# Token mixing of a two-block float32 layer stack: bonus products, off-block mask and output norm placed on GpSimd

## The reference, cut to what matters

```python
S = S * w_t + sa[..., None] * (kk_t * a_t) + v_t[..., None] * k_t      # the recurrence, token by token
y = ((y - mean) * rsqrt(var + 64e-5)).reshape(B, T, RW_WIDTH)          # norm of each head's 64 outputs
y = y * ln_x_w + ln_x_b
bonus = jnp.sum(r4 * k4 * r_k, axis=-1, keepdims=True) * v4            # one number per head and token, times v
y = (y + bonus) * g                                                    # g: the gate
```

## Time and profile before

| | |
|---|---|
| median of 3 runs | 3659.44 us (3657.07 to 3661.78) |
| the profiled execution | 3660.92 us, its span 3658.8 us |
| TensorE busy | 3543.9 us, 97% of the span |
| VectorE busy | 2155.3 us, 59% |
| ScalarE busy | 1755.6 us, 48% |
| GpSimd busy | 346.0 us, 9% |
| mean granted clock of TensorE over the span | 0.984 |
| token mixing's rounds | about 280 to 800 us of the span |

### The profile page before, as it was taken

How to read it: one execution, slowest core, us unless ns; L and a number is a source line. 1 busy time by engine, 2 the same in 40 slices (tenths; PEclk the granted TensorE clock), 3 DMA queues, 4 the chain that set the end, 5 groups by cost and what they waited for, 6 DMA issues and landing times. The chain is left out here.

```text
span 3658.8 us, 50852 instructions
## 1 busy us (share of the span) xinstructions
PE 3543.9 (97%) x20474; PEld 3010.5 (82%) x20474; DVE 2155.3 (59%) x2871; ACT 1755.6 (48%) x2613; POOL 346.0 (9%) x217
## 2 busy tenths in 40 slices
PE   8899999989999999999999999999999999999999
PEld 6777677678799999888899998887788887788777
DVE  4676556645566488555544465555687885555454
ACT  5454333324444478444444444444655554444753
POOL 0001000000059700000000000000022210000000
PEclk9999999999999999999999999999999999999999
DMA  6454234445545455555555565554533335455334
GB/s 224 157 183 153 97 137 141 146 169 199 199 168 179 178 171 180 186 211 188 190 207 184 207 254 193 219 191 176 182 141 138 133 132 186 176 195 185 127 138 161
DMA packets 112140, 638.57 MB, mean 175 GB/s; under 512 B 18698, under 2 KB 24618, under 8 KB 40152
## 3 DMA queue, kind: packets, MB, share of 16 engines
q1 hardware_dynamic: 106664, 622.98, 47.8%
q0 software_dynamic: 5296, 13.15, 1.1%
HBM read 611.10 MB, written 21.54 MB: 173 GB/s over the span
## 5 line engine op out<-in xcount | busy, mean ns | idle before, releaser
L222 DVE TENSOR_TENSOR lo_w<-ring,hi_w 128x1024 fp32r<-128x1024 f32 x500 | 612.6, 1225 | 987.4 <-ACT hi_w L216 979.2
L216 ACT CAST hi_w<-ring 128x1024 fp32r<-128x1024 f32 x540 | 569.8, 1055 | 954.2 <-DMA ring<-in_wstream 929.8
L224 DVE TENSOR_TENSOR lo_w<-ring,hi_w 128x1024 fp32r<-128x1024 f32 x500 | 612.3, 1225 | 0.0
L1997 PE MATMUL PS<-hi_x,lo_w 128*128 128x256 f32 x2048 | 580.1, 283 | 0.0
L1997 PE MATMUL PS<-hi_x,hi_w 128*128 128x256 f32 x2048 | 576.3, 281 | 3.0 <-POOL lo_w L224 3.0
L1997 PE MATMUL PS<-lo_x,hi_w 128*128 128x256 f32 x2048 | 571.4, 279 | 0.0
L217 ACT CAST hi_w<-ring 128x1024 fp32r<-128x1024 f32 x540 | 565.5, 1047 | 0.0
L2023 PE MATMUL PS<-hi_w,hi_g 128*128 128x512 f32 x1024 | 404.0, 395 | 1.3 <-issue 1.3
L2023 PE MATMUL PS<-lo_w,hi_g 128*128 128x512 f32 x1024 | 403.5, 394 | 0.0
L2023 PE MATMUL PS<-hi_w,lo_g 128*128 128x512 f32 x1024 | 403.2, 394 | 0.0
L1997 PEld LDWEIGHTS PS<-hi_x,hi_w 128*128 128x128 f32 x2048 | 389.2, 190 | 3.5 <-ACT GG L2237 3.4
(11 more groups left out here) (581 smaller groups left out, 5777.0 us busy)
## 6 DMA issues: line engine op xcount, KB each, us to landing
ring<-in_wstream SPq DMA_DIRECT2D x540, 1024.0 KB, 4.8
other_G<-staged SPq DMA_DIRECT2D x32, 256.0 KB, 6.1
hot<-other_G SPq DMA_DIRECT2D x8, 1024.0 KB, 6.9
gates_dram<-gst POOLq DMA_DIRECT2D x8, 512.0 KB, 4.8
x_dram<-x SPq DMA_DIRECT2D x2, 2048.0 KB, 12.0
x<-x_dram SPq DMA_DIRECT2D x2, 2048.0 KB, 9.4
prev<-RKV POOLq DMA_DIRECT2D x6, 508.0 KB, 5.2
x<-in_x SPq DMA_DIRECT2D x4, 512.0 KB, 6.6
```

The lines of the kernel that those rows point to most:

```text
L216: a.copy(hi_w[s][:, 0:HALF], ring[s][:, 0:HALF]).then_inc(S(f"hi{s}"), 1)
L222: v.tensor_tensor(lo_w[s][:, 0:HALF], ring[s][:, 0:HALF], hi_w[s][:, 0:HALF].bitcast(F32), ALU.subtract)
L224: v.tensor_tensor(lo_w[s][:, HALF:UNIT], ring[s][:, HALF:UNIT], hi_w[s][:, HALF:UNIT].bitcast(F32), ALU.subtract)\
L1997: m = nc.tensor.matmul(PS[:, s, 0:T], wa[s][:, k * P:(k + 1) * P], xa[:, k, :], start=(k == 0 and p == 0), stop=(k == KC - 1 and p == 2))
```

## The change

GpSimd computes the two bonus products of every round (`bonus_terms`, at the whole unit from offset 2.5), applies the mask (`off_block`, now in GpSimd's queue right behind `clear`, ahead of the gate copy or shift of the same unit), and, for rounds 0 to 2, computes the norm's five products and sums (`norm_lines`, at the whole unit from offset 16.25). On VectorE, `bonus` keeps the sum per head and moves from offset 4 to 7.25, behind the solve; the second half of the norm becomes `deviation` (a reciprocal, at the old place) and `gate_y` (the product with the gate, at offset 19.75, which is 7.75 of the next round). Round 3 keeps `finish`. The transpose of round 2's output moves from unit 77 to unit 80 on TensorE, ScalarE and VectorE, and the load of the second half of the norm's lines on SyncE from unit 66 to 68.

```diff
@@ SyncE
                 if u == 66:
                     gups(1)
+                if u == 68:
                     lines(1)
@@ TensorE
-                    if u == WIN + 1 and g < 3:
+                    if u == WIN + 1 and g < 2:
                         turn_y(g)
+                    if (u, g) == (WIN + 4, 2):
+                        turn_y(2)
@@ ScalarE
                     for n in late_due(U, g, 16, 13):
-                        a.wait_ge(S("gn_var"), n + 1)
+                        a.wait_ge(S("gn_var"), 2 * n + 1)
@@ GpSimd
+            def bonus_terms(n):
+                g.wait_ge(S("ends"), n + 1)
+                g.tensor_tensor(k4[:], k4[:], rkv_of(n)[0], ALU.mult)
+                g.drain()
+                g.tensor_tensor(k4[:], k4[:], par[:, 2, :], ALU.mult)
+                g.drain().then_inc(S("pool_terms"), 1)
+
+            def off_block(n):
+                g.wait_ge(S("rw_in"), 48)
+                g.tensor_tensor(LM[:, :, 0, :], LM[:, :, 0, :], offm[:].unsqueeze(1).broadcast_to((P, NH, P)), ALU.mult)
+                g.drain().then_inc(S("L_off"), 1)
+
+            def norm_lines(n):
+                r_, y_, v_ = rkv_of(n)
+                g.wait_ge(S("gn_var"), 2 * n + 2)
+                g.tensor_tensor(h3(r_), h3(v_), per_head(3 + n % 2), ALU.mult)
+                g.tensor_tensor(h3(y_), h3(y_), per_head(5), ALU.mult)
+                g.wait_ge(S("ln_in"), 32 * (n // 2) + 32)
+                g.drain()
+                g.tensor_tensor(y_, y_, lwlb[:, 0, :], ALU.mult)
+                g.drain()
+                g.tensor_tensor(y_, y_, lwlb[:, 1, :], ALU.add)
+                g.drain()
+                g.tensor_tensor(y_, y_, r_, ALU.add)
+                g.drain().then_inc(S("pool_terms"), 1)
...
                     if u == math.ceil(RB + RSTEP * n + 3.6):
                         steps_in(n)
                         clear(state_of(n, 1), "K_zero")
+                        off_block(n)
+                    if n < 3 and u == math.ceil(RB + RSTEP * n + 16.25):
+                        norm_lines(n)
+                    if u == math.ceil(RB + RSTEP * n + 2.5):
+                        bonus_terms(n)
                     if u == math.ceil(RB + RSTEP * n + 6.5):
                         steps_back(n)
@@ VectorE
             def bonus(n):
-                tt_(k4[:], k4[:], rkv_of(n)[0], ALU.mult)
-                v.drain()
-                tt_(k4[:], k4[:], par[:, 2, :], ALU.mult)
-                v.drain()
+                v.wait_ge(S("pool_terms"), (1, 2, 4, 6)[n])
                 v.tensor_reduce(s8[:, 3 + n % 2, :], h3(k4[:]), X, ALU.add)
                 v.drain().then_inc(S("bonus"), 1)
-            def off_block(n):
...
+            def deviation(n):
+                v.wait_ge(S("gn_std"), n + 1)
+                v.reciprocal(s8[:, 5, :], s8[:, 6, :])
+                v.drain().then_inc(S("gn_var"), 1)
+
+            def gate_y(n):
+                r_, y_, v_ = rkv_of(n)
+                v.wait_ge(S("pool_terms"), 2 * n + 3)
+                v.wait_ge(S("gt_ps"), n + 1)
+                tt_(r_, y_, PS[:, 3, :], ALU.mult)
+                v.drain().then_inc(S("y_done"), 1)
...
-                    for n in due(U, g, 4):
-                        bonus(n)
                     for n in late_due(U, g, 15.75, 12.75):
                         center(n)
                     for n in late_due(U, g, 16.25, 13.25):
-                        finish(n)
-                    for n in due(U, g, 5.25):
-                        off_block(n)
+                        if n < 3:
+                            deviation(n)
+                        else:
+                            finish(n)
                     for k in range(3):
                         for n in due(U, g, 6 + k / 4):
                             solve(n, k)
+                    for n in due(U, g, 7.25):
+                        bonus(n)
+                    for n in due(U, g, 19.75):
+                        if n < 3:
+                            gate_y(n)
...
-                    if U == WIN + 1 and g:
+                    if U == WIN + 1 and g in (1, 2):
                         turned_y(g - 1)
+                    if (U, g) == (WIN + 4, 3):
+                        turned_y(2)
```

More of the change, by code:

```diff
@@ L1606, in finish @@
                 v.wait_ge(S("gt_ps"), n + 1)
-                tt_(r_, y_, PS[:, 3 if n < 3 else 6, :], ALU.mult)
+                tt_(r_, y_, PS[:, 6, :], ALU.mult)
+                v.drain().then_inc(S("y_done"), 1)
[8 more added lines that the diff above has]
+                tt_(r_, y_, PS[:, 3, :], ALU.mult)
                 v.drain().then_inc(S("y_done"), 1)
```

## The result

The changed kernel takes 3682.65 us (median of 4, 3679.61 to 3685.88), the kernel before in the same comparison 3659.94 (median of 4). The ratio is 1.0061, with a 95% interval of 1.0048 to 1.0074: slower by 22.7 us. The profiled execution took 3683.94 us, with a span of 3682.1 and a granted clock of 0.981.

The account below looks back on a forecast made before the run. TensorE, busy 97%, was taken as the bound, waiting only where VectorE's bursts outlast the units split ahead. Rounds 0 to 3 summed as 3.9 + 4.3 + 7.3 + 1.0 = 16.5 us slower, 3676 on the median, range 3656 to 3689.

Parts of the forecast that it names:

- (c): Splits and solves: a 128x512 GpSimd product costs a two-input VectorE operation about 1.0 us, a 128x1024 one about 2.1.
- Whole-instruction exclusion: Skill's rule for GpSimd reads against two-input VectorE operations: each norm product would cost 1.3, the sum near 21 us.
- (c), last sentences: Later copy-in of norm lines on SyncE and copies back on GpSimd: microseconds to spare, closest in round 2.
- (a): Bonus reduction and previous round's gate moved behind the solve: 0.8 us each; costs 0.8, 0.5, 1.1 in rounds 0 to 2.
- The bonus products: On GpSimd they push one split by up to 1.0 us, ahead of a 1.2 TensorE wait: nothing.
- lost cover: If the 1.2 us TensorE wait covering the split delayed by bonus products were gone: 1.0 us a round.
- (b): Round 0's mask ahead of the shift's copy in GpSimd's queue: 3.1 us, bounds 2.4 and 4.2.
- Round 3: Freed time pays for mask and two products; three more cost 2.85, the missing turned block gives 0.85: 1.0 us later.
- No contention: Rival: GpSimd's turns fall into VectorE's idle time; +1.5 us, 3661, no change; chance 0.19.
- Faster: Rival: VectorE's own queue sets the solve's start, so freed time removes waits; 15 us less, 3644; chance 0.13.
- Worse: Rival: GpSimd runs at blocked length, norm outlasts the solve, and TensorE's clock falls after long waits; 3689; chance 0.08.
- likeliest case: Contention as summed over the four rounds: 16.5 us slower, own range 3667 to 3684; chance 0.60.

Follow-up runs that it names:

- pars_early: The changed kernel with SyncE's load of the second half's parameters waiting for GpSimd's bonus products instead of VectorE's sum; 3674.11 us, ratio 1.0037.
- round3_vector: The kernel before, nothing on GpSimd, with round 3's bonus and mask behind its solve and the third turned block moved as in the change; 3658.28 us, ratio 0.9990.
- norm_back: The changed kernel with the norm's second half back on VectorE for all rounds, GpSimd keeping bonus products and mask; 3665.09 us, ratio 1.0014.
- norm_writes: The changed kernel with GpSimd's five norm products and sums of rounds 0 to 2 replaced by memsets of the same tiles; 3662.52 us, ratio 1.0005.
- keys_late: The kernel before with round 3's bonus and mask behind its solve, and in rounds 1 to 3 keys_norm moved behind the spread; 3651.07 us, ratio 0.9974.

## Why the prediction was right, and where it was not

The direction and the mechanism held: slower, by contention in splits and solve. The sum was 16.5 us, measured was 22.7, of which 20.2 lie in the four rounds.

- *Contention, (c).* The forecast had 3, 4 and 3 held products in the solves of rounds 1, 2 and 3, at 0.95 each; there were 3, 3 and 1. The solves of rounds 1 and 2 took 12.8 us against 10.0 and 10.4, so about 0.9 and 0.8 each (a held product took 1.07 to 1.15, where the same one alone takes 0.18 to 0.22). Whole-instruction exclusion, the rule that was weighed there, describes what happens: a held product ends when GpSimd's operation ends. The price was nevertheless below the 1.29 of the operation: in the rows above VectorE spends the first part of each GpSimd operation in a reduction that is not held. The sum of near 21 us that this rule gave is closer than mine to the 20.2 of the rounds, but by chance: up to 4.8 us of the 20.2 come from the wait on SyncE, which is no contention. Round 2's stretch was forecast to lose 7.3 in all and lost 6.8; round 1, without the SyncE wait, 3.7 against 4.3. I named the solve at 13 to 14 us; it was a little less.
- *The missed wait, (c), last sentences.* The prediction looked at the norm lines on SyncE and not at `pars(1)`, which stands in the same queue and waits for `bonus`, the very signal that (a) moves from ahead of the solve to behind it. Everything behind `pars(1)` in that queue waited too, two ring loads among it. pars_early puts it at 3.1 us, and up to 1.7 more by the clock. This is the step of the prediction that failed.
- *The bonus products, put at nothing.* They cost 1.1 us in round 0: a split of 2.29 pushed `masked`, and TensorE waited. The price for a lost cover, 1.0 a round, was right; the cover was missing in round 0.
- *(b), 3.1 us for the mask in round 0.* The copy was issued some 2.8 us later against the start of the values, as forecast, but landed sooner: 4.2 us after its issue at 342.43, against 6.2 after 337.85 before. In the six kernels with the mask ahead of the shift the solve starts 22.4 to 24.3 us after the values (mean 23.4), in the seven others 21.8 to 22.8 (mean 22.3). So its place costs about 1.1 us, an estimate from two groups that overlap. The rest is made up by the copy: from its issue to VectorE's going on there were 4.2 to 5.7 us in the first group and 5.9 to 7.1 in the second; why is open. In the changed kernel itself the solve starts 0.8 later than before; with the sum's 0.8 and the late second shift's 1.0 this gives 2.6 of the 2.9 us that round 0's stretch lost. The 0.65 for a drain was also too much (0.17 here).
- *Round 3.* 1.0 forecast, 0.8 measured, and the bank wait of 10.8 lies in the 8 to 11 named. The two sides of the balance are real: the freed time is worth 2.9 in round3_vector, and the norm on GpSimd costs 2.2 by norm_back. How they were put together was not right, and that the sum fits is in part luck. The solve was to start 0.9 us earlier than before and to hold three products; measured from the values it starts 1.2 later, since the four split halves ahead of it lose some 5 us, and it holds one product, 0.9 us.
- *Rivals.* No contention is refuted by norm_writes against the changed kernel. Faster is refuted: with the norm written and not read, rounds 1 and 2 still stay above those of before, and from the values to the solve's start they take 17.9 and 18.9 us against 18.5 and 18.7, so the freed time hardly moves the solve. Worse did not come about as put, since the norm ended long before the solve; but the clock's fall behind a long wait, which was in that rival, is to be seen in round 1.

The rounds exceed the sum by 3.7 us: 3.1 and 1.7 missed in round 1, 0.4 more in round 0, less 0.6, 0.7 and 0.2 by which the rest of rounds 1, 2 and 3 was oversized. The remaining 2.5 us to the medians are 0.7 ahead of round 0 and the spread of the later part. The measured 3682.65 lies near the upper end of the likeliest case's own range of 3667 to 3684; pars_early, which is the change without the wait on SyncE, took 3674.11, near its middle.

## What to carry to other kernels

A GpSimd operation that reads SBUF is not free beside a busy VectorE: each small two-input operation of a dependent chain that it meets ends with GpSimd's. Give GpSimd arithmetic only where VectorE reduces, copies from PSUM or waits: the two copies `turned_k` from PSUM took 1.29 us beside GpSimd's first bonus product in round 0 and 1.29 before the change. When a signal moves to a later place, list every queue that waits for it and what stands behind that wait; here one semaphore on SyncE cost as much as three or four held products. And where a burst of VectorE's work sets a wait, look first for an item that can go behind it: that gave 9 us here (keys_late), and the move to another engine gave nothing.

## What I had not expected of the hardware

- GpSimd's product with one number per head took 1.05 us over 128x512, with two full tiles 1.29 to 1.30; a memset 0.53 to 0.55.
- A GpSimd drain behind a product left a gap of 0.15 to 0.17 in the rows of the norm and the mask, and of 0.24 to 0.57 behind the first bonus product, less than the 0.65 that I took from the earlier trace rows.
- The 60 matmuls ahead of a round, with no wait among them, took either 16.4 or 13.2 us in both kernels. Before, for the stretches ahead of rounds 1 and 3:

```profile
409.54:425.93 16.39, 16.39 (x60) 8.88 (x58) 2.07 (x3) 4.89 (x8) 0.00 (x0) 0.69 0.03 4
645.88:659.06 13.18, 13.18 (x60) 7.84 (x58) 1.66 (x3) 4.89 (x8) 0.00 (x0) 0.87 0.03 4
```

and after:

```profile
414.53:427.77 13.24, 13.24 (x60) 7.81 (x58) 1.66 (x3) 4.88 (x8) 0.00 (x0) 0.87 0.07 9
662.77:679.15 16.38, 16.38 (x60) 8.89 (x57) 1.89 (x3) 4.88 (x8) 0.00 (x0) 0.69 0.03 4
```

The same matmuls and no idle time; only the granted clock differs, 0.69 or 0.87, means over a stretch that was partly at 1.2 and partly at 2.4 GHz. A single stretch can thus look 3 us better or worse with nothing changed; here one went each way and the sum was untouched. What decides it was not tried.
